# Queries and 92 expert tiles as pairs of seven half products, and the spread stage with the 36 tiles that are left

## The reference

```python
def peer_ffn(h, w_pq, sub_keys, u_emb, v_emb):
    q = (h @ w_pq).reshape(b, s, PEER_HEADS, 2, PEER_HALF)          # 8 heads, 2 x 128
    ...
    sc = jnp.einsum('bshpc,pnc->bshpn', q, sub_keys)                # 128 keys a half
    top_v, top_i = lax.top_k(sc, PEER_TOPK)                         # 16 a half
    cand = top_v[..., 0, :, None] + top_v[..., 1, None, :]          # 16 x 16
    best_v, best_i = lax.top_k(cand, PEER_TOPK)
    expert = i1 * PEER_KEYS + i2                                    # one of 16384
    gate = jax.nn.softmax(best_v, axis=-1)
    ...
    a = jnp.einsum('bthkd,btd->bthk', u_emb[expert], h)
    act = jax.nn.gelu(a) * gate
    return jnp.einsum('bthk,bthkd->btd', act, v_emb[expert])
```

## Time and profile before

| | |
|---|---|
| median of 3 runs | 5091.68 us (5091.26 to 5094.24) |
| time of the profiled execution | 5093.29 us |
| its span | 5091.6 us |
| mean granted clock of PE | 0.962 |
| PE | 4756.0 us, 93% |
| DVE | 2591.5 us, 51% |
| ACT | 1628.5 us, 32% |
| POOL | 1247.9 us, 25% |
| DMA | mean 109 GB/s |

### The profile page before, as it was taken

How to read it: one execution, slowest core, us unless ns; L and a number is a source line. 1 busy time by engine, 2 the same in 40 slices (tenths; PEclk the granted TensorE clock), 3 DMA queues, 4 the chain that set the end, 5 groups by cost and what they waited for, 6 DMA issues and landing times. The chain is left out here.

```text
span 5091.6 us, 64130 instructions
## 1 busy us (share of the span) xinstructions
PE 4756.0 (93%) x22416; PEld 3785.5 (74%) x22416; DVE 2591.5 (51%) x4079; ACT 1628.5 (32%) x2585; POOL 1247.9 (25%) x754
## 2 busy tenths in 40 slices
PE   6999999976988979999989999999799999999998
PEld 5666666644767758888868888888588888888886
DVE  3777777784514235646554444444344444444445
ACT  3555555553413322222223333333211111111111
POOL 1444434431114112212212111211122222222221
PEclk8999999978989979999999999999899999999999
DMA  2111111104432122222224444444644444344341
GB/s 76 38 42 47 46 47 46 38 17 157 153 120 83 56 102 79 83 74 86 79 84 156 148 148 151 154 148 148 227 165 148 144 148 141 138 144 148 140 148 67
DMA packets 260924, 555.78 MB, mean 109 GB/s; under 512 B 15664, under 2 KB 146992, under 8 KB 258608
## 3 DMA queue, kind: packets, MB, share of 16 engines
q1 hardware_dynamic: 260784, 554.01, 31.9%
HBM read 384.60 MB, written 169.35 MB: 109 GB/s over the span
## 5 line engine op out<-in xcount | busy, mean ns | idle before, releaser
L149 PE MATMUL expert_o<-expert_ahi,expert_vhi 128*128 128x512 f32 x2048 | 798.9, 390 | 35.0 <-POOL expert_vlo L2007 30.1
L151 PE MATMUL expert_o<-expert_ahi,expert_vlo 128*128 128x512 f32 x2048 | 797.9, 390 | 0.0
L150 PE MATMUL expert_o<-expert_alo,expert_vhi 128*128 128x512 f32 x2048 | 797.9, 390 | 0.0
L2071 DVE TENSOR_TENSOR expert_acc<-expert_acc,expert_o 128x512 f32<-128x512 f32 x496 | 341.1, 688 | 710.2 <-PE expert_o L151 705.5
L1387 POOL TENSOR_TENSOR ulo<-uraw,uhi 128x1024 fp32r<-128x1024 f32 x128 | 311.7, 2436 | 1373.6 <-ACT uhi L1383 1373.6
L2007 POOL TENSOR_TENSOR expert_vlo<-expert_vraw,expert_vhi 128x1024 fp32r<-128x1024 f32 x128 | 323.1, 2525 | 1053.1 <-ACT expert_vhi L2025 1053.1
L149 PE MATMUL spread_a<-hhi,uhi 128*128 128x512 f32 x1280 | 505.5, 395 | 15.1 <-POOL ulo L1387 15.1
L151 PE MATMUL spread_a<-hhi,ulo 128*128 128x512 f32 x1280 | 499.5, 390 | 0.0
L150 PE MATMUL spread_a<-hlo,uhi 128*128 128x512 f32 x1280 | 498.6, 390 | 0.0
L149 PEld LDWEIGHTS expert_o<-expert_ahi,expert_vhi 128*128 128x128 f32 x2048 | 385.1, 188 | 117.2 <-issue 36.4
L1862 DVE TENSOR_TENSOR spread_one<-spread_iota,spread_parts 128x2048 f16<-128x2048 f16 x64 | 184.0, 2875 | 527.5 <-PE spread_g L1886 526.8
(11 more groups left out here) (289 smaller groups left out, 8596.9 us busy)
## 6 DMA issues: line engine op xcount, KB each, us to landing
uraw<-in_peer_u SPq DMA_DIRECT2D x128, 512.0 KB, 4.1
gelu_u<-ugelu SPq DMA_DIRECT2D x128, 512.0 KB, 2.9
gates<-spread_stage SPq DMA_DIRECT2D x16, 4096.0 KB, 17.3
expert_act<-gelu_u SPq DMA_DIRECT2D x128, 512.0 KB, 3.6
expert_graw<-gates SPq DMA_DIRECT2D x128, 512.0 KB, 4.4
expert_vraw<-in_peer_v SPq DMA_DIRECT2D x128, 512.0 KB, 6.6
mix_w_raw<-in_w_mix SPq DMA_DIRECT2D x56, 512.0 KB, 3.7
xattn_w_raw<-in_w_cross SPq DMA_DIRECT2D x32, 512.0 KB, 3.6
```

The costliest lines, as they stand in the source:

```text
L149: nc.tensor.matmul(out, whi, xhi, start=(first and i == 0), stop=False)
L150: nc.tensor.matmul(out, whi, xlo, start=False, stop=False)
L151: mm = nc.tensor.matmul(out, wlo, xhi, start=False, stop=(last and i == len(terms) - 1))
L2071: nc.vector.tensor_tensor(acc[:, k, h * H:h * H + H], acc[:, k, h * H:h * H + H], ops[:, d, h], ALU.add).then_inc(added, 1)
```

## The change

Two tiles (256 rows) are taken as a pair, and the product of a pair with h is done by Strassen's scheme in Winograd's form: the weights of a pair are four blocks, each tile's first and second half of the channels (`raw`, 512 columns each), h is four quarters, and seven products (`PairProducts.product`, j = 0 to 6) of 12 matmuls each replace eight. This goes for 54 pairs in the select phase: 8 of queries and 46 of experts (92 tiles). What is new for it:

- GpSimd makes four sums of weight blocks per pair (`sums`), then four groups of low parts (`low`), in place of one low part per tile. ScalarE makes the high parts in four groups (`high`), copies product 0 out of PSUM (`copy_first`), and applies GELU in place in SBUF. DVE adds the products in SBUF: seven additions per pair (`add`), placed by hand between the pieces of its work for the heads.
- Before the first pair DVE makes four sums of quarters of h and their low parts; the quarter that the sums overwrite goes out to `h12` and is read back and split during the last pair.
- A pair is loaded as one transfer of 1 MB and stored as four of 256 KB.
- A head has six pairs; the query pair of the next head is its fourth. Behind the last head stand five pairs; in the second of them the 24 transposes are done, and ScalarE and DVE write `parts` for the spread phase at once, so that `sel` is gone.

The spread phase has 36 tiles: four per block, eight in the last. A block begins with three tiles, then come steps 0 and 1, half a tile, steps 2 and 3, half a tile, steps 4 to 7, and what is left. `one1` and `gate` have three buffers; the second one-hot is made in the place of the gate's low part, which costs one more wait inside a step. The stage is stored as it lies, [block, token, key, expert], in four transfers per block that ScalarE's queue issues behind its last copy of a block; each is 2 MB in runs of 16 KB. ScalarE waits for them before its first copy of the next block. The expert phase reads the gates of a tile back in runs of 512 B.

```diff
-SELECT_TILES = 48
+PAIRS_PER_HEAD = 6
+QUERY_AT = 3
+TAIL_PAIRS = 5
+SELECT_TILES = 92
...
+    def load(self, sync, n):
+        if n >= 2:
+            sync.wait_ge(self.done, self.NP * (n - 2) + 5)
+        sync.dma_start(self.raw[:, n % 2].rearrange("p b n -> p (b n)"),
+                       self.pairs_in[n].rearrange("p a c n -> p (a c n)")).then_inc(self.loaded[n % 2], 16)
+
+    def sums(self, pool, n, m, s):
+
+        a, g = self.raw[:, s], self.nc.gpsimd
+        pool.wait_ge(self.loaded[s], m * 16 + 16)
+        g.tensor_tensor(a[:, 2], a[:, 0], a[:, 2], ALU.subtract).then_inc(self.sum_made, 1)
+        if not (isinstance(n, int) and n == 0):
+            pool.wait_ge(self.done, n * self.NP - 4)
+        pool.wait_ge(self.sum_made, n * 4 + 1)
+        g.tensor_tensor(self.s2[:], a[:, 3], a[:, 2], ALU.subtract).then_inc(self.sum_made, 1)
+        pool.wait_ge(self.sum_made, n * 4 + 2)
+        g.tensor_tensor(self.s14[:, s, 0], a[:, 0], self.s2[:], ALU.add).then_inc(self.sum_made, 1)
+        g.tensor_tensor(self.s14[:, s, 1], a[:, 1], self.s2[:], ALU.subtract).then_inc(self.sum_made, 1)
...
+    def groups(self, s):
+
+        return ((self.raw[:, s, 0:2], self.hi[:, 0:2], self.raw_low[:, s, 0:2]), (self.s2[:], self.hi[:, 4], self.s2_low[:]),
+                (self.raw[:, s, 2:4], self.hi[:, 2:4], self.raw_low[:, s, 2:4]),
+                (self.s14[:, s], self.hi[:, 5:7], self.s14_low[:, s]))
+
+    def low(self, pool, n, s, g):
+        src, high, low = self.groups(s)[g]
+        if g == 0:
+            pool.wait_ge(self.sum_made, n * 4 + 4)
+        pool.wait_ge(self.hi_made, n * 4 + (g + 1))
+        self.nc.gpsimd.tensor_tensor(low, src, high.bitcast(F32), ALU.subtract).then_inc(self.lo_made, 1)
+
+    def high(self, act, n, m, s, g):
+
+        src, high, _ = self.groups(s)[g]
+        if g == 0:
+            act.wait_ge(self.loaded[s], m * 16 + 16)
+        else:
+            act.wait_ge(self.sum_made, n * 4 + (2, 2, 4)[g - 1])
+        if not (isinstance(n, int) and n == 0):
+            act.wait_ge(self.done, n * self.NP - (5, 4, 2, 0)[g])
+        self.nc.scalar.activation(high, src, ACT.Copy).then_inc(self.hi_made, 1)
...
+    def copy_first(self, act, n):
+        act.wait_ge(self.done, n * self.NP + 1)
+        act.wait_ge(self.freed[0], n * 16 + 1)
+        self.nc.scalar.activation(self.block(0), self.ps[:, 0], ACT.Copy).then_inc(self.copied, 1)
+
+    def activate(self, act, n, c):
+        act.wait_ge(self.added, n * self.NP + (2, 7, 4, 6)[c])
+        self.nc.scalar.activation(self.block(c), self.block(c), ACT.Gelu_apprx_tanh).then_inc(self.gelu, 1)
+
+    def product(self, pe, n, s, j, made=None):
+
+        first = isinstance(n, int) and n == 0
+        if j != 1:
+            group = (0, None, 1, 2, 2, 3, 3)[j]
+            pe.wait_ge(self.lo_made, n * 4 + (group + 1))
+        if j == 0 and not first:
+            pe.wait_ge(self.added, n * self.NP - 3)
+        if j == 1 and not first:
+            pe.wait_ge(self.added, n * self.NP - 1)
+        if j == 2 and not first:
+            pe.wait_ge(self.added, n * self.NP)
+        if j == 3 and not first:
+            pe.wait_ge(self.added, n * self.NP - 4)
+        if j == 4:
+            pe.wait_ge(self.copied, n + 1)
+        if j == 5:
+            pe.wait_ge(self.added, n * self.NP + 2)
+        if j == 6:
+            pe.wait_ge(self.added, n * self.NP + 1)
+        bank = (0, 1, 2, 3, 0, 1, 2)[j]
+        high = self.hi[:, (0, 1, 4, 2, 3, 5, 6)[j]]
+        low = (self.raw_low[:, s, 0], self.raw_low[:, s, 1], self.s2_low[:], self.raw_low[:, s, 2], self.raw_low[:, s, 3],
...
+        bank = (0, 1, 2, 3, 0, 1, 2)[j]
+        high = self.hi[:, (0, 1, 4, 2, 3, 5, 6)[j]]
+        low = (self.raw_low[:, s, 0], self.raw_low[:, s, 1], self.s2_low[:], self.raw_low[:, s, 2], self.raw_low[:, s, 3],
+               self.s14_low[:, s, 0], self.s14_low[:, s, 1])[j]
+        b_hi, b_lo = [(h[:, 0], h[:, 2], t[:, 1], t[:, 2], h[:, 1], t[:, 0], h[:, 3])[j]
+                      for h, t in ((self.h_hi, self.t_hi), (self.h_lo, self.t_lo))]
+        for k in range(4):
+            if made:
+                pe.wait_ge(*made(k))
+            kp = slice(k * P, k * P + P)
+            mm = three_pass(self.nc, self.ps[:, bank], [(high[:, kp], low[:, kp], b_hi[:, k], b_lo[:, k])],
+                            first=(k == 0), last=(k == 3))
+        mm.then_inc(self.done, 1)
...
+    def add(self, dve, n, j):
+
+        tt, c, ps, count = self.nc.vector.tensor_tensor, self.block, self.ps, n * self.NP
+        dve.wait_ge(self.done, count + (j + 1))
+        if j == 2:
+            dve.wait_ge(self.copied, n + 1)
+            dve.wait_ge(self.freed[1], n * 16 + 1)
+            tt(c(1), c(0), ps[:, 2], ALU.add).then_inc(self.added, 1)
+            dve.wait_ge(self.added, count + 1)
+            tt(c(0), c(0), ps[:, 1], ALU.add).then_inc(self.added, 1)
+        elif j == 3:
+            dve.wait_ge(self.freed[3], n * 16 + 1)
+            dve.wait_ge(self.added, count + 1)
+            tt(c(3), c(1), ps[:, 3], ALU.add).then_inc(self.added, 1)
+        elif j == 4:
+            dve.wait_ge(self.freed[2], n * 16 + 1)
+            dve.wait_ge(self.added, count + 3)
+            tt(c(2), c(3), ps[:, 0], ALU.subtract).then_inc(self.added, 1)
+        elif j == 5:
+            tt(c(1), c(1), ps[:, 1], ALU.add).then_inc(self.added, 1)
+            dve.wait_ge(self.added, count + 4)
+            tt(c(3), c(3), ps[:, 1], ALU.add).then_inc(self.added, 1)
+        else:
+            dve.wait_ge(self.added, count + 5)
+            tt(c(1), c(1), ps[:, 2], ALU.add).then_inc(self.added, 1)
+
...
+def pair_kinds():
+
+    kinds = [0]
+    for hd in range(PH):
+        for i in range(PAIRS_PER_HEAD):
+            kinds.append(hd + 1 if i == QUERY_AT and hd < PH - 1 else None)
+    return kinds + [None] * TAIL_PAIRS
...
+            dve.wait_ge(hlo_made, NC)
+            tt(B22, B22, B12, ALU.subtract).then_inc(t_made, 1)
+            dve.wait_ge(h12_stored, 16)
+            dve.wait_ge(t_made, 1)
+            tt(B12, B12, B11, ALU.subtract).then_inc(t_made, 1)
+            dve.wait_ge(t_made, 2)
+            tt(B11, B22, B11, ALU.add).then_inc(t_made, 1)
+            dve.wait_ge(t_made, 3)
+            tt(B21, B11, B21, ALU.subtract).then_inc(t_made, 1)
+            for x in range(4):
+                t_low(x)
...
+            def pair(n, m_next, s_next, kind, more=True, between=None):
+
+                pr.copy_first(act, n)
+                if more:
+                    pr.high(act, n + 1, m_next, s_next, 0)
+                if kind is None:
+                    pr.activate(act, n, 0)
+                if more:
+                    pr.high(act, n + 1, m_next, s_next, 1)
+                if between:
+                    between()
+                if more:
+                    pr.high(act, n + 1, m_next, s_next, 2)
+                if kind is None:
+                    pr.activate(act, n, 2)
+                    pr.activate(act, n, 3)
+                if more:
+                    pr.high(act, n + 1, m_next, s_next, 3)
+                if kind is None:
+                    pr.activate(act, n, 1)
...
+                add(2, 2)
+                find_second(3, 8)
+                add(2, 3)
+                find_second(8, 14)
+                add(2, 4)
+                find_second(14, 16)
+                dve.wait_ge(index8, hd * NU + NU)
+                alone(dve, index16, hd * NU + NU + 1)
+                candidates(0, 3)
+                add(2, 5)
+                candidates(3, 8)
+                add(2, 6)
+                nc.vector.tensor_copy(idxf[:], idx[:]).then_inc(idxf_made, 1)
+                alone(dve, cand_made, hd * NT + NT)
+                candidate_best(0, 4)
+
...
+                positions(hd)
+                hits(hd, 0)
+
+                add(5, 2)
+                hits_index(hd, 0)
+                add(5, 3)
+                hits_sum(hd, 0)
+                add(5, 4)
+                hits(hd, 1)
+                add(5, 5)
+                hits_index(hd, 1)
+                add(5, 6)
+                hits_sum(hd, 1)
...
+    def load(self, sync, n):
+        if n >= 3:
+            sync.wait_ge(self.done, 2 * (n - 3) + 2)
+        sync.dma_start(self.raw[:, n % 3], self.u_stream[n]).then_inc(self.loaded[n % 3], 16)
+
+    def store(self, sync, tile0, n, h):
+        sync.wait_ge(self.gelu, 2 * n + h + 1)
+        sync.dma_start(self.a_out[tile0 + n, :, h * H:h * H + H], self.out[:, h]).then_inc(self.stored[h], 16)
+
+    def split_high(self, act, n):
+        act.wait_ge(self.loaded[n % 3], n // 3 * 16 + 16)
+        if n >= 2:
+            act.wait_ge(self.done, 2 * (n - 2) + 2)
...
+        PER = 4
+        FIRST, BETWEEN = 6, 2
+        TILES = KEYS - SELECT_TILES
+        NS = 4
...
+        def halves(tt):
+
+            count = PER if tt < NT - 1 else TILES - PER * (NT - 1)
+            every = [(tt * PER + i // 2, i % 2) for i in range(2 * count)]
```

(37 more changed lines are left out.)

720 lines of the change are left out of this document (401 added, 319 removed).

## The result

The changed kernel takes 5000.8 us (median; 4996.5 to 5003.6), the kernel before, run beside it, 5093.0 (5091.3 to 5096.4): ratio 0.9814, with an interval of 0.9801 to 0.9826. The profiled execution has a span of 5001.8 us, 89.8 less than before. The forecast was 5039, a gain of 53.

A forecast was written before the change was run, and what follows sets the result against it. The prediction took the number of TensorE matmuls to bound select and spread. Its terms, -147 + 18 + 16 - 5 + 72 - 10 + 3 = -53, took 5091.7 to 5039 us; stated range 4995 to 5088.

The forecast's parts named there:

- rival (a): Spread gate steps: DVE keeps up better, no meeting with GpSimd's low parts, clock stays up; 32 us, total 4999; chance 0.15.
- What bounds it, and the 147: Select and spread are bound by matmul count; 648 fewer matmuls at 0.227 us each save 147 us.
- The start, +18: Start of select: sums and low parts of h delay the first products; 18 us more, bounds 10 and 27.
- The pairs, +16: Running select pairs: DVE additions come about 1 us late twice a head; 16 us more, bounds 0 and 50.
- The scores, given as unchanged: Score matmuls in select were said to stay as they are, adding no time.
- The seam to spread, -5: Select to spread: gap falls from 23.2 to about 13.4 us, but transposes between products cost 5; net 5 us less.
- The gate steps, +72: Spread blocks: DVE is late for s6 and s7, 7.5 us plus 1.5 for the clock per block; 72 us more.
- its signs, at the end: Spread gates: about 8 times two PE waits of 3 and 1 us, with granted clock below 1, would show the 72.
- The gates' stores, 0: Spread: a block's 8.4 MB of gates land before the next block's s0, 33 us later; no cost.
- Rival (c): Spread: gates' stores land late, s0 waits 6 us and a slow stretch follows in 7 blocks; total 5079; chance 0.10.
- The seam to the expert stage, -10: Spread to expert stage: SyncE no longer stands behind gates' stores, 4.9 of 14.8 us left; 10 us less.
- The expert stage's first loads, +3: Expert stage start: gates read in 512 B runs slow the first four tiles; 3 us more, bounds 0 and 10.

The follow-up runs named there:

- sums-more runs: Changed kernel with GpSimd computing one sum of each select pair one, two or four times more: 5012.7, 5090.8 and 5202.1 us.
- five and three: Changed kernel with five half tiles ahead of a spread block's gate steps and three between them, instead of six and two: 4958.5 us, ratio 0.9735.

## Why the prediction came out as it did

The measured time is that of rival (a), but its mechanism did not come true: it gives 32 us for the gate steps, and they took 52. Most of the other 20 us came from terms that this rival had left alone, 15 of them from the pairs of select. That the time meets 4999 so closely is luck. What the forecast had right is which stages are bound by what, and in which steps PE waits; its terms for the pairs and for the gate steps were too large.

- **What bounds it, and the 147.** Right. From one product to the next PE has 0.2269 us a matmul in the pairs of select (504 in 114.35 us), a pair 19.04 us.
- **The start, +18.** Right: pair 0 ended 13.9 us later than the 96 matmuls that it replaces, and 2.7 of it are counted in the 147, so 16.6. Its wait for the first low part is 11.9 us; "about 12" was said.
- **The pairs, +16.** The term was too large: 1.0 us of waiting in place of 16. Collisions were more than followed, for casts collide as well, and what they cost was less, since they came off slack in nearly every pair. What was wrong is where the slack was looked for. The working followed the additions; the sums-more runs show the tight place at GpSimd's first low part, with 2.0 us. The scores, given as unchanged, take about 0.6 us a head more, 5 in all.
- **The seam to spread, -5.** The gap is 13.2 us where 13.4 was worked out (the four parts named there add up to 12.8); the transposes between products cost 3, not 5.
- **The gate steps, +72.** Right in mechanism, place (s6 and s7) and shape (five and three removes it, smaller low parts remove most), too large in size: periods of 64.8 us, 66.3 in the first two, against 66.3 + 1.5, or 52 us in eight blocks. Of the 20 too many, some 10 are the clock, taken at 1.5 us a block from the earlier trace rows: it fell in six blocks of eight, but in four of these the slow matmuls only filled the wait for s7, as the prediction had half said, and it cost 3 us in all. The other 10 are the step, 4.79 us where 5.1 was put for the added wait: waits of 2.2 and 2.8 us for s6 and s7 where its timeline gives 3.4 and 3.2 (its signs, at the end, say 3 and 1, which does not follow from that timeline). Rival (a) had supposed that the low parts don't meet the chain. They do, each time. Smaller low parts would have given 30 of the 40 us that it promised (3.8 in eight blocks).
- **The gates' stores, 0.** Right: a block's last store lands 24 to 25.4 us behind the first issue. Rival (c) fell for the changed kernel, and the run with three half tiles ahead shows what lateness costs. What carried the term was underrated: "runs of 16 KB should not be slower" is true of the transfer, but the larger part, 17 us a block, is the time that ScalarE is held while the four are issued. The four issues take 3.1 us, where 0.4 each was said.
- **The seam to the expert stage, -10.** Right in size (20.1 us against 30.1), wrong in cause. It was put down to ScalarE's queue; with SyncE issuing the same stores the seam is 20.8 us, and with the old layout 20.1. What is left of the differences is the closeness: before, two transfers of gates were issued 21 and 8 us ahead of the last expert output, whose issue was held for 8.05 us; the second of them landed at 3651.2, the output at 3652.5, and the first load of the expert stage went out at 3654.3. After, eight half tiles, 43 us, lie between. No run puts the closeness back alone, so this cause is inferred, not shown; four half tiles, in the run with one more pair, were still enough.
- **The expert stage's first loads, +3.** 1.2 us.

In sum: -147 + 17 + 1 + 5 - 10 + 3 + 52 - 10 + 1 = -88, against -89.8 in the spans. The forecast erred by counting three unknown costs (collisions in select, clock, step) each at a value on the dear side, 15, 10 and 10 us; they add up in one direction, and all the rest, the 5 of the scores aside, is within 2 us of its term.

## What to carry to other kernels

Give each engine's list its due times, and find the place with the least slack for every engine that feeds the bound one, not only for the one you think of: below the slack a collision costs nothing; above it an added 1.3 us a pair cost 12 us in this kernel and 2.6 us cost 90. Where a short chain must be ready in bursts, place the bound engine's other work in between before making the chain faster: one constant gave 42 us. Cost a store by the number of its pieces, charge it to the next issue of the same engine, and ask what that engine has to compute behind it. Keep large stores out of the queue in which small ones stand that someone waits for.

## What the runs showed of the hardware

- Of four stores of 2 MB issued in a row, each in 4096 pieces of 512 B, the first held its engine for 0.4 us, the second for 5.4 and the others for 7.3 each, 20.4 in all on ScalarE and 20.5 on SyncE; in 128 pieces of 16 KB four took 3.1 us.
- A 256 KB store took 10.3 us to land beside 8.4 MB in another queue and 17.1 behind them in its own; the next one took 13.4 to 15.0 in either case.
- DVE's casts of 256 elements, with a single input, took 2.5 and 2.05 us beside GpSimd where they had taken 0.30: not only operations with two SBUF inputs are held. The Trainium skill, "SBUF — State Buffer", section "Who interferes with whom", has an operation of DVE contend with GpSimd if it has two SBUF inputs or runs in a two-port mode, which a cast can do; the casts fit the second case, though no view shows the mode.
- The clock after idle time is not set by one wait's length. Waits of 2.21 us for s6 and 2.83 for s7 left it at 1.00 in two blocks of the changed kernel (3183 and 3248); in the other six, with the same 2.21 us, the window at s6 and s7 or the one behind it had 0.59 to 0.73. In the run with SyncE's queue the window at s6 and s7 had 1.00 in three blocks and 0.56 to 0.72 in five; one of these:

```profile
3253.00:3259.00 6.00, 3.50 (x39) 3.24 (x40) 5.93 (x6) 2.30 (x4) 0.00 (x0) 0.62 0.00 0
```

What decides stays open. A fall of the clock costs nothing where the engine would have waited anyway.
